# Output projection and gate by result blocks: the last two weight tiles accumulate one 128x512 quarter after the other, and a transpose moves behind the first attention tile

## The chip, the cores and the metric

The kernel runs on one core of a Trainium2 chip. Its time is the device time of one execution in microseconds (us). The engines are TensorE (PE, with its weight loads shown apart as PEld), VectorE (DVE), ScalarE (ACT), GpSimd (POOL) and SyncE (SP), which here only issues DMAs. Each works through its own queue in order and waits on semaphores. PE writes its results to PSUM, which has eight banks of 512 fp32 columns on 128 partitions.

## The reference: what is computed

Two layers on 256 tokens of width 1024. In each layer:

```
h  = rmsnorm(x);  f = h @ w_in + b_in
attn = rmsnorm(sliding_window_attention(f))          # 512 channels
rw   = rwkv7(f): recurrence, group norm, gate        # 512 channels
x  = x + concat[attn, rw] @ w_out                    # output projection
x  = x + peer(rmsnorm(x))                            # 8 heads, top 16 of 128^2 experts
x  = x + (p @ ple_proj) * sigmoid(rmsnorm(x) @ ple_gate)   # gate
```

and a last rmsnorm on the output.

## The kernel before, in words

**Precision and weight tiles.** Every large product is made of three fp32r matmuls, high x high, high x low and low x high, where a weight tile (128x1024) is split into `high` (an ACT cast, L456) and `low` (a DVE or POOL subtraction, L827, L426) and the activations into `hTh` and `hTl`. Weight tiles lie two to a 1 MB slab in a ring of four slabs, which SP fills in order; a slab is loaded when the `low` parts of the slab before it in its place have been made. `high` and `low` have four buffers (`DEEP = 4`), and the tile with number `count` may be cast only when `part_used` says that PE is done with the tile four before it. The tiles in their order within a layer: `in` 0 to 20, `out` 0 to 7, `wq` 0 to 15, 256 expert tiles, `ple` 0 to 9 (two for `p @ ple_proj`, eight for the gate).

**Row projections.** The output projection and the gate both run through `token_rows` (L1315). For each weight tile it waits for the tile's `low` part and issues 12 matmuls of 512 columns (L1327): for both token tiles (128 tokens each) the three products, each into two banks. The result thus lies in four blocks of 128x512, in banks 0 to 3 (n = 0, 1 are token tile 0), and all four are complete only with the last weight tile. `p @ ple_proj` lies in banks 4 to 7.

**Output projection.** Out tiles 0 to 3 multiply the attention's channels, 4 to 7 the recurrence's. PE transposes the recurrence's output for tokens 0 to 127 (`transpose_y(0)`), runs out tiles 0 to 3, transposes tokens 128 to 255 (`transpose_y(1)`, L1549) and releases DVE by `yT_ps`. DVE has the low parts of out tiles 4, 5 and 6 in its queue ahead of its wait for `yT_ps`; then it makes `ytmp` for two channel pairs (L1057 to L1062), ACT casts each (L625), DVE makes each `hTl` (L1066). PE waits for the first `hTl` (`yTr_ready`), runs out tiles 4 and 5, waits for the second and runs 6 and 7. DVE adds the four blocks to `xres` (L1074) after a single wait for the last tile, with the low parts of wq 0 to 2 ahead of that wait.

**Norm.** ACT squares and sums each token tile of `xres` (L465) when `x_ready` has counted its additions, POOL makes the reciprocal root (L395, L396), DVE scales (L832), PE transposes 16 squares of 128x128 (L1292), two to an eviction of ACT (`hTh`, L472) and of DVE (`hTl`, L838). ACT can begin when both token tiles' first channels are transposed. Both engines' `norm` take a function `meanwhile` (tile splits) that they run ahead of their evictions. Behind it PE's `channel_rows` (L1301) runs the `wq` or the next layer's `in` tiles: 24 matmuls of 256 columns (L1311) into one bank.

**Gate.** PE runs `ple` tiles 0 and 1 on `p`, the norm, then tiles 2 to 9. ACT waits once for the last tile and makes four sigmoids (L806), DVE for each block a product (L1271) and an addition to `xres` (L1272). In layer 0 both have the split of the next layer's `in` tile 0 in their queues ahead of that; ACT casts `in` 1 and 2 behind the sigmoids.

The order of every queue is written out by hand. The one wait that the sigmoids have, for example, is

```
act.wait_ge(part_used, projection_tile(L, "ple", KT + 1).count + 1)
```

Of the kernel before, what the change touches and what calls it, by code (L numbers as in the profile page):

```python
# [15 lines left out]
P = 128  # L16
DEPTH, SEQ, D = 2, 256, 1024
TB = SEQ // P
KT = D // P
# [33 lines left out]
DEEP = 4  # L53
# [10 lines left out]
C_GMIX, C_GFFN, C_GPLE, C_BIN, C_MU = 0, 8, 16, 24, 45  # L64
# [70 lines left out]
def hybrid_encoder(nc, x, w_slabs, peer_slabs, vecs, consts, p_t, g_final, out):  # L135
    with ExitStack() as ctx:
        def sem(name):
            return ctx.enter_context(nc.semaphore(name))
# [127 lines left out]
        sumsq, rms, xn_ready, xT_ps, hT_hi, hT_lo = (sem(n) for n in ("sumsq", "rms", "xn_ready", "xT_ps", "hT_hi", "hT_lo"))  # L266
        x_ready = sem("x_ready")

# [174 lines left out]
        def _(act):  # L443
# [7 lines left out]
            def split(tile):  # L451

                if tile.count >= DEEP:
                    act.wait_ge(part_used, tile.count - DEEP + 1)
                act.wait_ge(filled[tile.slab % RING], 16 * fills(tile.layer, tile.slab))
                act.copy(high[:, tile.count % DEEP], raw(tile.slab, tile.half)).then_inc(part_hi, 1)  # L456
# [17 lines left out]
            for L in range(DEPTH):  # L474
                V = vec[:, L]

                def early():
                    if L:
                        split(projection_tile(L, "in", 3))
                    else:  # L480
                        for k in range(2):
                            split(projection_tile(L, "in", k))
                        act.wait_ge(in_v, 16)

                norm(3 * L, V[:, C_GMIX:C_GMIX + KT], early)
                if L == 0:
                    for k in range(2, 4):
                        split(projection_tile(L, "in", k))
                if L == 0:
# [136 lines left out]
                split(projection_tile(L, "out", KT - 1))  # L626
                for k in range(4):
                    split(projection_tile(L, "wq", k))

                norm(3 * L + 1, V[:, C_GFFN:C_GFFN + KT])  # L630

# [170 lines left out]
                if L < DEPTH - 1:  # L802
                    split(projection_tile(L + 1, "in", 0))
                act.wait_ge(part_used, projection_tile(L, "ple", KT + 1).count + 1)
                for n in range(4):
                    act.activation(sgm[:, n // 2, (n % 2) * 512:(n % 2 + 1) * 512], PS[:, n], ACT.Sigmoid).then_inc(sgm_ready, 1)  # L806
                if L < DEPTH - 1:
                    for k in range(1, 3):
                        split(projection_tile(L + 1, "in", k))

# [4 lines left out]
        def _(dve):  # L815
# [28 lines left out]
            for L in range(DEPTH):  # L844
# [223 lines left out]

                for k in range(3):
                    split(projection_tile(L, "wq", k))  # L1070
                dve.wait_ge(part_used, projection_tile(L, "out", KT - 1).count + 1)
                for n in range(4):
                    s = slice((n % 2) * 512, (n % 2 + 1) * 512)
                    ins = dve.tensor_tensor(xres[:, n // 2, s], xres[:, n // 2, s], PS[:, n], ALU.add)  # L1074
                    if n % 2:
                        ins.then_inc(x_ready, 1)
                dve.wait_ge(x_ready, TB * (3 * L + 1))

                norm(3 * L + 1, V[:, C_GFFN:C_GFFN + KT], lambda: split(projection_tile(L, "wq", 3)))

# [184 lines left out]
                if L < DEPTH - 1:  # L1265
                    split(projection_tile(L + 1, "in", 0))
                dve.wait_ge(part_used, projection_tile(L, "ple", KT + 1).count + 1)
                for n in range(4):
# [15 lines left out]
        def _(pe):  # L1284
# [30 lines left out]
            def token_rows(L, stage, k0, hi, lo, ktiles, bank0, norm=None, first=True, last=True):  # L1315

                for k in range(ktiles):
                    tile = projection_tile(L, stage, k0 + k)
                    pe.wait_ge(low_dve, tile.low + 1)
                    if norm is not None:  # L1320

                        pe.wait_ge(hT_lo, KT * (norm + 1))
                    b = tile.count % DEEP
                    for tb in range(TB):
                        for c, (h, w) in enumerate(((hi, high), (hi, low), (lo, high))):
                            for s in range(2):
                                ins = mm(PS[:, bank0 + 2 * tb + s], h[:, k, tb * P:(tb + 1) * P], w[:, b, s * 512:(s + 1) * 512],  # L1327
                                         start=first and k == 0 and c == 0, stop=last and k == ktiles - 1 and c == 2)
                    ins.then_inc(part_used, 1)

            pe.wait_ge(in_c, 16)
            pe.wait_ge(zeros_made, 1)
            for L in range(DEPTH):
# [221 lines left out]

                pe.wait_ge(y_ready, NCHUNK * (L + 1))
                token_rows(L, "out", 0, hTh, hTl, 4, 0, last=False)
                transpose_y(1, yT_ps)
                for n in range(2):
                    pe.wait_ge(yTr_ready, 2 * L + n + 1)  # L1560
                    ks = slice(4 + 2 * n, 6 + 2 * n)
                    token_rows(L, "out", 4 + 2 * n, hTh[:, ks], hTl[:, ks], 2, 0, first=False, last=n == 1)

# [113 lines left out]
                norm(3 * L + 2)  # L1677
                token_rows(L, "ple", 2, hTh, hTl, KT, 0, 3 * L + 2)

# [95 lines left out]
```

## Time and profile before

| | |
|---|---|
| median of 3 runs | 2297.89 us (2294.98 to 2299.03) |
| the profiled execution | 2296.89 us, span of its instructions 2295.1 us |
| busy: PE / DVE / ACT / POOL | 2184.8 / 1604.7 / 1102.1 / 329.4 us |
| chain that ended last, by engine | PE 79%, DVE 7%, POOL 6%, issue 6%, ACT 1% |
| mean granted clock of TensorE | 0.979 |

How to read it: the span goes from the first instruction to the last. The chain is followed back from the last instruction, at each step to what released it. "x48" is a number of instructions; a bracket behind a row of a timeline is the idle time of the engine before it and what ended that.
### The profile page before, as it was taken

To read this page: it belongs to the slowest core of one execution; us is meant where nothing else is said; L and a number is where in the kernel's file an instruction comes from. 1 tells how busy PE (TensorE), PEld (TensorE's weight loads), DVE (VectorE), ACT (ScalarE), POOL (GpSimd) and SP (SyncE) were. 2 spreads that over 40 slices of the span, in tenths; PEclk is the share of its full clock that TensorE was granted. 3 is DMA by queue.
4 is the path that set the end of the run, shared out by engine and by line. 5 is a ranking of instruction groups with operands and counts; after the bars stand their busy time and mean duration, and the time that the engine had idled before them with its cause. 6 is when DMAs were issued, how large, how long until landed. Compare 5 with 4: busy or idle time off the path is not lost.

```text
span 2295.1 us, 55123 instructions
## 1 busy us (share of the span) xinstructions
PE 2184.8 (95%) x21760; PEld 1948.0 (85%) x21760; DVE 1604.7 (70%) x3080; ACT 1102.1 (48%) x1891; POOL 329.4 (14%) x164
## 2 busy tenths in 40 slices
PE   8897999999999999999898889999999999999997
PEld 8786999988888888788696869999888888887885
DVE  6645697786666667975566448978766666679754
ACT  5533455444444444445464334554444444445443
POOL 0020698000000000000000216970000000000000
PEclk9899999999999999999998989999999999999998
DMA  6212345434444444445341123544344444444451
GB/s 250 92 40 75 129 166 184 145 129 164 164 166 167 168 171 157 159 159 190 127 149 73 40 92 129 178 170 147 129 164 164 164 166 166 169 158 154 166 193 63
DMA packets 46617, 335.03 MB, mean 146 GB/s; under 512 B 5168, under 2 KB 5296, under 8 KB 6320
## 3 DMA queue, kind: packets, MB, share of 16 engines
q1 hardware_dynamic: 46512, 333.61, 40.5%
q8 instruction: 68, 1.11, 0.2%
q14 instruction: 37, 0.30, 0.0%
HBM read 332.54 MB, written 1.05 MB: 145 GB/s over the span
## 4 chain that ended last, share of the span: by engine, by line
PE 79%; DVE 7%; POOL 6%; issue 6%; ACT 1%; DMA 0%; POOLq 0%; SPq 0%; DVEq 0%; ACTq 0%
PE PS L1626 31%; PE PS L1603 23%; PE PS L1311 8%; PE PS L1615 6%; POOL low L432 5%; PE PS L1327 4%; PE PS L1518 1%; PE PS L1475 1%; DVE low L1084 1%; PE PS L1509 1%; PE PS L1299 1%; DVE rnorm L943 1%; DVE hot L1154 1%; DVE hot L1150 1%; PE PS L1343 0%
## 5 line engine op out<-in xcount | busy, mean ns | idle before, releaser
L651 ACT CAST high<-ring 128x1024 fp32r<-128x1024 f32 x512 | 535.6, 1048 | 602.7 <-PE PS L1603 444.4
L1603 PE MATMUL PS<-hTh,high 128*128 128x256 f32 x2048 | 594.7, 290 | 12.7 <-ACT GA L655 10.9
L1603 PE MATMUL PS<-hTh,low 128*128 128x256 f32 x2048 | 578.8, 283 | 0.0
L1603 PE MATMUL PS<-hTl,high 128*128 128x256 f32 x2048 | 577.2, 282 | 0.0
L1084 DVE TENSOR_TENSOR low<-ring,high 128x1024 fp32r<-128x1024 f32 x432 | 515.5, 1220 | 0.8 <-ACT high L651 0.6
L1603 PEld LDWEIGHTS PS<-hTh,high 128*128 128x128 f32 x2048 | 387.2, 189 | 17.4 <-ACT GA L655 9.7
L1603 PEld LDWEIGHTS PS<-hTl,high 128*128 128x128 f32 x2048 | 387.5, 189 | 0.0
L1603 PEld LDWEIGHTS PS<-hTh,low 128*128 128x128 f32 x2048 | 387.5, 189 | 0.0
L1626 PE MATMUL PS<-high,WH 128*128 128x512 f32 x1024 | 323.8, 397 | 0.0
L1626 PE MATMUL PS<-low,WH 128*128 128x512 f32 x1024 | 318.0, 392 | 0.0
L1626 PE MATMUL PS<-high,WL 128*128 128x512 f32 x1024 | 316.4, 390 | 0.0
L1147 DVE TENSOR_TENSOR is_i<-iota_half,repeats 128x256 bf16<-128x256 bf16 x256 | 74.3, 290 | 256.4 <-ACT repeats L681 252.3
L395 POOL TENSOR_SCALAR stat<-stat 128x1 f32<-128x1 f32 x14 | 5.0, 356 | 1638.4 <-ACT xn L465 1638.4
L432 POOL TENSOR_TENSOR low<-ring,high 128x1024 fp32r<-128x1024 f32 x80 | 226.4, 2867 | 32.7 <-ACT high L651 32.7
L1626 PEld LDWEIGHTS PS<-high,WL 128*128 128x128 f32 x1024 | 192.2, 188 | 43.0
L1626 PEld LDWEIGHTS PS<-low,WH 128*128 128x128 f32 x1024 | 192.2, 188 | 42.9
L1615 PEld LDWEIGHTS PS<-hot,hot 128*128 128x128 bf16 x6144 | 169.9, 96 | 60.1 <-issue 54.1
L1626 PEld LDWEIGHTS PS<-high,WH 128*128 128x128 f32 x1024 | 179.2, 188 | 26.4
L1615 PE MATMUL PS<-hot,hot 128*128 128x32 bf16 x6144 | 193.9, 177 | 7.6 <-DVE hot L1154 7.6
L672 ACT CAST WH<-GA 128x256 fp32r (+1 forms) x256 | 102.7, 401 | 201.4 <-PE PS L1626 190.9
L1150 DVE TENSOR_TENSOR hot<-iota_half,repeats 128x1024 bf16<-128x1024 bf16 x256 | 175.6, 686 | 0.0
L1311 PE MATMUL PS<-hTh,high 128*128 128x256 f32 x592 | 173.3, 293 | 2.4 <-DVE hTl L838 2.4
(245 smaller groups left out, 3020.5 us busy)
## 6 DMA issues: line engine op xcount, KB each, us to landing
ring<-in_peer_slabs SPq DMA_DIRECT2D x256, 1024.0 KB, 4.8
ring<-in_w_slabs SPq DMA_DIRECT2D x58, 1024.0 KB, 4.8
xres<-in_x SPq DMA_DIRECT2D x2, 512.0 KB, 4.6
out<-obuf SPq DMA_DIRECT2D x2, 512.0 KB, 2.6
cst<-in_consts SPq DMA_DIRECT2D x1, 680.0 KB, 10.5
praw<-in_p_t SPq DMA_DIRECT2D x1, 512.0 KB, 15.1
gfin<-in_g_final SPq DMA_DIRECT2D x1, 512.0 KB, 5.6
vec<-in_vecs SPq DMA_DIRECT2D x1, 356.0 KB, 7.3
```

What stands on the lines that cost most here:

```text
L432: pool.tensor_tensor(low[:, b], ring[:, place, half * D:(half + 1) * D], high[:, b].bitcast(F32), ALU.subtract).then_inc(low_pool, 1)
L651: act.copy(high[:, (c0[L] + j) % DEEP], ring[:, place, half * D:(half + 1) * D]).then_inc(part_hi, 1)
L672: act.copy(WH[:, j % 2:j % 2 + 1], GA[:, bass.ds(place, 1)]).then_inc(w_hi, 1)
L943: dve.reciprocal(rnorm[:], rnorm[:]).then_inc(kk_ready, 1)
L1084: dve.tensor_tensor(low[:, b], ring[:, place, half * D:(half + 1) * D], high[:, b].bitcast(F32), ALU.subtract).then_inc(low_dve, 1)
L1147: dve.tensor_tensor(is_i2[:, b].rearrange("p t (a c) -> p t a c", c=REP), iotas[:, QT // REP * chunk:QT // REP * (chunk + 1)].unsqueeze(1) ...
L1150: dve.tensor_tensor(hot1[:, b].rearrange("p t (a c) -> p t a c", c=REP), iotas.unsqueeze(1).broadcast_to([P, GROUP, NSUB // REP, REP]), re ...
L1311: ins = mm(dst, w[:, b, ks], h[:, k], start=n == 0, stop=n == 3 * KT - 1)
L1327: ins = mm(PS[:, bank0 + 2 * tb + s], h[:, k, tb * P:(tb + 1) * P], w[:, b, s * 512:(s + 1) * 512], start=first and k == 0 and c == 0, sto ...
L1603: ins = mm(PS[:, 6 + j % 2, 0:SEQ], u[:, b, ks], h[:, k], start=n == 0, stop=n == 3 * KT - 1)
L1615: ins = mm(PS[:, 4 + b, t * QT:(t + 1) * QT], hot1[:, b, t], hot2[:, b, part, t], start=part == 0, stop=part == 2)
L1626: ins = mm(PS[:, 2 * tb + s], w[:, j % 2, tb * P:(tb + 1) * P], v[:, b, s * 512:(s + 1) * 512], start=False, stop=False, skip_group_check= ...
```

## The change

1. **Output projection, order on PE.** Out tile 0, then `transpose_y(1)`, then out tiles 1 to 3, where the transposes stood behind tile 3.
2. **Last two tiles by blocks.** A new function `block_after_block` runs the last two weight tiles of the output projection and of the gate. It waits for the later tile's `low` part once and then, for each of the four blocks, issues the six matmuls of both tiles. Each of the first three blocks has a semaphore count (`out_ps`, `gate_ps`); with the last block both tiles count as used (`part_used`). The number of matmuls and of weight loads is as before. For the output projection both halves of `hTl` are now awaited ahead of the first block; each of tiles 4 and 5 still waits for the first half alone.
3. **DVE and ACT, block by block.** DVE waits for each block ahead of its addition, ACT for each block ahead of its sigmoid.
4. **Splits moved.** `wq` 2 and 3 can be cast only when the blocks are done: ACT casts them in the norm, between the squares and the evictions; DVE makes the low part of `wq` 2 there and that of `wq` 3 behind its evictions. In the gate of layer 0, ACT casts `in` 1 and 2 of the next layer between the next norm's squares and evictions, and `in` 3 behind the evictions; DVE's order there is unchanged.

```diff
--- before.py
+++ after.py
@@ -264,7 +264,7 @@
         zeros_made = sem("zeros_made")
 
         sumsq, rms, xn_ready, xT_ps, hT_hi, hT_lo = (sem(n) for n in ("sumsq", "rms", "xn_ready", "xT_ps", "hT_hi", "hT_lo"))
-        x_ready = sem("x_ready")
+        x_ready, out_ps, gate_ps = (sem(n) for n in ("x_ready", "out_ps", "gate_ps"))
 
         bq_ready, in_evac, mixed = (sem(n) for n in ("bq_ready", "in_evac", "mixed"))
         vtA_ps, vtA_ready, sc_ps, lg_made, nm_ready, p_ready = (sem(n) for n in ("vtA_ps", "vtA_ready", "sc_ps", "lg_made", "nm_ready", "p_ready"))
@@ -476,16 +476,16 @@
 
                 def early():
                     if L:
-                        split(projection_tile(L, "in", 3))
+                        for k in range(1, 3):
+                            split(projection_tile(L, "in", k))
                     else:
                         for k in range(2):
                             split(projection_tile(L, "in", k))
                         act.wait_ge(in_v, 16)
 
                 norm(3 * L, V[:, C_GMIX:C_GMIX + KT], early)
-                if L == 0:
-                    for k in range(2, 4):
-                        split(projection_tile(L, "in", k))
+                for k in range(3 if L else 2, 4):
+                    split(projection_tile(L, "in", k))
                 if L == 0:
                     act.wait_ge(in_p, 16)
                     act.copy(pTh[:], praw[:]).then_inc(p_hi, 1)
@@ -624,10 +624,14 @@
                     act.wait_ge(yg_ready, 2 * L + n + 1)
                     act.copy(hTh[:, 4 + 2 * n:6 + 2 * n], ytmp[:, 2 * n:2 * n + 2]).then_inc(yTr_hi, 1)
                 split(projection_tile(L, "out", KT - 1))
-                for k in range(4):
+                for k in range(2):
                     split(projection_tile(L, "wq", k))
 
-                norm(3 * L + 1, V[:, C_GFFN:C_GFFN + KT])
+                def rest():
+                    for k in range(2, 4):
+                        split(projection_tile(L, "wq", k))
+
+                norm(3 * L + 1, V[:, C_GFFN:C_GFFN + KT], rest)
 
                 def scores_out(m):
                     act.wait_ge(psc_ps, HC * L + m + 1)
@@ -801,12 +805,12 @@
                 act.activation(ahead, minus_half, ACT.Sigmoid)
                 if L < DEPTH - 1:
                     split(projection_tile(L + 1, "in", 0))
-                act.wait_ge(part_used, projection_tile(L, "ple", KT + 1).count + 1)
                 for n in range(4):
+                    if n < 3:
+                        act.wait_ge(gate_ps, 3 * L + n + 1)
+                    else:
+                        act.wait_ge(part_used, projection_tile(L, "ple", KT + 1).count + 1)
                     act.activation(sgm[:, n // 2, (n % 2) * 512:(n % 2 + 1) * 512], PS[:, n], ACT.Sigmoid).then_inc(sgm_ready, 1)
-                if L < DEPTH - 1:
-                    for k in range(1, 3):
-                        split(projection_tile(L + 1, "in", k))
 
             norm(3 * DEPTH, None)
 
@@ -1066,17 +1070,21 @@
                     dve.tensor_tensor(hTl[:, ks], ytmp[:, 2 * n:2 * n + 2], hTh[:, ks].bitcast(F32), ALU.subtract).then_inc(yTr_ready, 1)
                 split(projection_tile(L, "out", KT - 1))
 
-                for k in range(3):
+                for k in range(2):
                     split(projection_tile(L, "wq", k))
-                dve.wait_ge(part_used, projection_tile(L, "out", KT - 1).count + 1)
                 for n in range(4):
                     s = slice((n % 2) * 512, (n % 2 + 1) * 512)
+                    if n < 3:
+                        dve.wait_ge(out_ps, 3 * L + n + 1)
+                    else:
+                        dve.wait_ge(part_used, projection_tile(L, "out", KT - 1).count + 1)
                     ins = dve.tensor_tensor(xres[:, n // 2, s], xres[:, n // 2, s], PS[:, n], ALU.add)
                     if n % 2:
                         ins.then_inc(x_ready, 1)
                 dve.wait_ge(x_ready, TB * (3 * L + 1))
 
-                norm(3 * L + 1, V[:, C_GFFN:C_GFFN + KT], lambda: split(projection_tile(L, "wq", 3)))
+                norm(3 * L + 1, V[:, C_GFFN:C_GFFN + KT], lambda: split(projection_tile(L, "wq", 2)))
+                split(projection_tile(L, "wq", 3))
 
                 def split_tile(count, j, place, half):
                     dve.wait_ge(part_hi, c0[L] + 1 + count)
@@ -1264,7 +1272,6 @@
                     split(projection_tile(L, "ple", k))
                 if L < DEPTH - 1:
                     split(projection_tile(L + 1, "in", 0))
-                dve.wait_ge(part_used, projection_tile(L, "ple", KT + 1).count + 1)
                 for n in range(4):
                     s = slice((n % 2) * 512, (n % 2 + 1) * 512)
                     dve.wait_ge(sgm_ready, 4 * L + n + 1)
@@ -1327,6 +1334,22 @@
                                 ins = mm(PS[:, bank0 + 2 * tb + s], h[:, k, tb * P:(tb + 1) * P], w[:, b, s * 512:(s + 1) * 512],
                                          start=first and k == 0 and c == 0, stop=last and k == ktiles - 1 and c == 2)
                     ins.then_inc(part_used, 1)
+
+            def block_after_block(L, stage, k0, hi, lo, done):
+
+                tiles = [projection_tile(L, stage, k0 + k) for k in range(2)]
+                pe.wait_ge(low_dve, tiles[1].low + 1)
+                for n in range(4):
+                    rows, cols = slice(n // 2 * P, (n // 2 + 1) * P), slice(n % 2 * 512, (n % 2 + 1) * 512)
+                    for k, tile in enumerate(tiles):
+                        b = tile.count % DEEP
+                        mm(PS[:, n], hi[:, k, rows], high[:, b, cols], start=False, stop=False)
+                        mm(PS[:, n], hi[:, k, rows], low[:, b, cols], start=False, stop=False)
+                        ins = mm(PS[:, n], lo[:, k, rows], high[:, b, cols], start=False, stop=k == 1)
+                        if n == 3:
+                            ins.then_inc(part_used, 1)
+                    if n < 3:
+                        ins.then_inc(done, 1)
 
             pe.wait_ge(in_c, 16)
             pe.wait_ge(zeros_made, 1)
@@ -1554,12 +1577,13 @@
 
 
                 pe.wait_ge(y_ready, NCHUNK * (L + 1))
-                token_rows(L, "out", 0, hTh, hTl, 4, 0, last=False)
+                token_rows(L, "out", 0, hTh, hTl, 1, 0, last=False)
                 transpose_y(1, yT_ps)
-                for n in range(2):
-                    pe.wait_ge(yTr_ready, 2 * L + n + 1)
-                    ks = slice(4 + 2 * n, 6 + 2 * n)
-                    token_rows(L, "out", 4 + 2 * n, hTh[:, ks], hTl[:, ks], 2, 0, first=False, last=n == 1)
+                token_rows(L, "out", 1, hTh[:, 1:4], hTl[:, 1:4], 3, 0, first=False, last=False)
+                pe.wait_ge(yTr_ready, 2 * L + 1)
+                token_rows(L, "out", 4, hTh[:, 4:6], hTl[:, 4:6], 2, 0, first=False, last=False)
+                pe.wait_ge(yTr_ready, 2 * (L + 1))
+                block_after_block(L, "out", 6, hTh[:, 6:8], hTl[:, 6:8], out_ps)
 
                 norm(3 * L + 1)
 
@@ -1675,7 +1699,8 @@
                     pe.wait_ge(p_lo, 1)
                 token_rows(L, "ple", 0, pTh[:, L], pTl[:, L], 2, 4)
                 norm(3 * L + 2)
-                token_rows(L, "ple", 2, hTh, hTl, KT, 0, 3 * L + 2)
+                token_rows(L, "ple", 2, hTh, hTl, KT - 2, 0, 3 * L + 2, last=False)
+                block_after_block(L, "ple", KT, hTh[:, KT - 2:KT], hTl[:, KT - 2:KT], gate_ps)
 
 
 def shape_constants():
```

## Rows read from the trace of the kernel before

**Rows 1.** The chain that ended last, share of the span by line (page).

```profile
PE PS L1626 31%; PE PS L1603 23%; PE PS L1311 8%; PE PS L1615 6%; POOL low L432 5%; PE PS L1327 4%; PE PS L1518 1%; PE PS L1475 1%; DVE low L1084 1%; PE PS L1509 1%; PE PS L1299 1%; DVE rnorm L943 1%; DVE hot L1154 1%; DVE hot L1150 1%; PE PS L1343 0%
```

**Rows 2.** Waits, whole span: waiter, releaser: total us, times, longest.

```profile
...
PE PS L1292 <- DVE xn L832: 24.3, 6, 8.0
...
PE PS L1327 <- DVE hTl L1066: 11.1, 2, 5.5
```

**Rows 3.** Chain, layer 0, output projection and norm: start us, us, what.

```profile
...
182.59 11.35 PE PS L1327 x48
193.94 0.96 PE PS L1549 x30
...
200.39 13.29 PE PS L1327 x48
...
218.04 2.36 PE PS L1292 x10
...
221.93 6.12 PE PS L1311 x48
```

**Rows 4.** Timeline, DVE, same stretch: start, us, operation, idle before.

```profile
...
184.15 0.43 DVE L1017 TENSOR_TENSOR yc<-yc,stat 128x256 f32<-128x256 f32 x1
...
192.27 1.23 DVE L827 TENSOR_TENSOR low<-ring,high 128x1024 fp32r<-128x1024 f32 x1 [1.56 <-ACT high L456]
194.93 0.99 DVE L1057 TENSOR_SCALAR ytmp<-PS,vec 128x256 f32<-128x256 f32 x2 [1.43 <-PE PS L1549]
...
209.21 1.23 DVE L827 TENSOR_TENSOR low<-ring,high 128x1024 fp32r<-128x1024 f32 x1 [1.56 <-ACT high L456]
...
213.70 2.48 DVE L1074 TENSOR_TENSOR xres<-xres,PS 128x512 f32<-128x512 f32 x4 [0.48 <-PE PS L1327]
```

**Rows 5.** Timeline, ACT, the same stretch.

```profile
...
213.70 1.04 ACT L456 CAST high<-ring 128x1024 fp32r<-128x1024 f32 x1 [1.74 <-PE PS L1327]
...
216.22 1.06 ACT L465 ACTIVATE xn<-xres 128x1024 f32<-128x1024 f32 x1
...
220.42 3.03 ACT L472 ACTIVATE hTh<-PS,vec 128x256 fp32r<-128x256 f32 x8 [3.06 <-PE PS L1292]
```

**Rows 6.** Timeline, DVE, layer 0's gate and the norm behind it.

```profile
...
1136.77 1.23 DVE L827 TENSOR_TENSOR low<-ring,high 128x1024 fp32r<-128x1024 f32 x1 [6.09 <-ACT high L456]
1140.28 0.69 DVE L1271 TENSOR_TENSOR ptmp<-sgm,PS 128x512 f32<-128x512 f32 x1 [2.29 <-ACT sgm L806]
...
1144.97 0.71 DVE L1272 TENSOR_TENSOR xres<-xres,ptmp 128x512 f32<-128x512 f32 x1
...
1147.86 0.75 DVE L832 TENSOR_SCALAR xn<-xres,stat 128x1024 f32<-128x1024 f32 x1 [1.39 <-POOL stat L396]
```

**Rows 7.** Chain, layer 1, output projection and norm.

```profile
...
1338.88 14.02 PE PS L1327 x48
...
1358.77 0.70 PE PS L1292 x2
...
1361.01 7.72 PE PS L1311 x48
```

**Rows 8.** DMA issues (page): KB each, us to landing.

```profile
...
ring<-in_w_slabs SPq DMA_DIRECT2D x58, 1024.0 KB, 4.8
```

**Rows 9.** Timeline, ACT, layer 0's gate.

```profile
...
1139.58 2.06 ACT L806 ACTIVATE sgm<-PS 128x512 f32<-128x512 f32 x4 [2.84 <-PE PS L1327]
```

**Rows 10.** Chain, layer 1's gate.

```profile
...
2257.53 24.93 PE PS L1327 x96
...
2287.88 0.70 DVE xres L1272
```

**Rows 11.** Windows: length; busy (instructions) by engine; granted clock; DMA share; GB/s.

```profile
...
218.00:222.00 4.00, 3.70 (x17) 3.33 (x17) 2.59 (x4) 1.58 (x5) 0.63 (x2) 0.57 0.13 16
222.00:258.00 36.00, 36.00 (x305) 36.00 (x305) 17.31 (x105) 17.30 (x34) 23.58 (x10) 1.00 0.39 145
```

**Rows 12.** Instructions of L1327: duration ns min/median/max, first and last start, forms.

```profile
...
L1327 PE MATMUL PS<-high,hTh x128: 390/395/796, 182.5 to 2281.1; 128*128 128x512 f32 x128
```

## The prediction

> **What bounds the kernel.** I read the chain of waits first. TensorE (PE) holds 79% of it, most in the expert stage (L1626, L1603) and the column projections (L1311), which the edit leaves alone [rows 1]. The table of waits then shows PE idle mainly in the norms, until VectorE (DVE) has scaled a token tile (24.3 us in six waits), and 11.1 us, in two, ahead of the last output-projection tiles [rows 2]. Nothing else covers such a pause, so what shortens one moves all that follows. I read the four places touched (output projection and gate of both layers) engine by engine. Below, E is the end of a projection's last matmul, E' its end after the change; "block" is one 128x512 quarter of the result.
>
> **Early transposes (twice).** In layer 0 PE takes 48 matmuls for four weight tiles in 11.35 us (0.2365 each, 2.84 a tile), transposes for 0.96, then waits until 200.39 [rows 3]. After the change the transposes stand behind tile 0, at 182.59 + 2.84 = 185.4. Their input is complete at 184.15 + 0.43 = 184.6, so they don't stall [rows 4]. The work is only moved. But DVE, first to read the transposes, has the low parts of out tiles 4 to 6 ahead of that in its queue. The last of these starts at 192.27 and takes 1.23; it follows ScalarE's (ACT) cast of that tile, which waits for PE to finish tile 2, and tile 2 now ends 0.96 later. So DVE is free at 192.27 + 1.23 + 0.96 = 194.46, where it now starts at 194.93 [rows 4]. Of the 5.5 us pause only 0.47 goes; the late thing next is DVE itself, whose seven steps up to the first hTl are unchanged. Nearest bounds: 0, and 1.43 if DVE's whole wait there went [rows 4]. I take 0.47, twice, 0.94 in all. The second wait, now ahead of the blocks, is long over: both hTl end at 201.1, two tiles before the blocks begin.
>
> **Output projection by blocks, with norm.** E is 200.39 + 13.29 = 213.68 in layer 0 [rows 3]. Blocks end at E' minus 4.26, 2.84, 1.42 and 0 (six matmuls of 0.2365). DVE's queue has the low part of wq tile 1 ahead of the additions: 209.21 + 1.23 - 0.47 = 209.97, which is E' - 3.24. Additions run at 0.62 (2.48 for four) [rows 4]: two end by E' - 1.9, the third by E' - 0.7, and only the fourth (0.68 to its end) stands behind E'. Now four stand there, with the two squares of ACT in a row behind the first pair: the second square starts at 216.22, E + 2.54 [rows 5]. After the change it starts at E' + 0.7.
>
> From the last update of xres to DVE's second scaling is 2.18 us, read where the first square is long done, as it will be here: 1144.97 + 0.71 to 1147.86 [rows 6]. So that scaling starts at E' + 2.88 and ends at E' + 3.63. Two transposes until ACT may read follow (0.70 in layer 1 [rows 7], which I take; ten in a row took 2.36 in layer 0 [rows 3], so 0.47 is the lower end). ACT starts at about E' + 4.39, and from there to PE's first wq matmul it was 221.93 - 220.42 = 1.51 [rows 3, 5]. That gives E' + 5.90, against 221.93 - 213.68 = 8.25 in layer 0 and 1361.01 - 1352.90 = 8.11 in layer 1 [rows 3, 7]. The eight transposes of the first token tile are ready from E' + 1.5 and done by E' + 3.4 at the 0.236 of layer 0's ten: covered. Saved: 2.35 and 2.21, sum 4.56.
>
> What is moved: tiles 6 and 7 now free their buffers together, at E', so ACT's casts of wq 2 and 3 (1.04 each [rows 5]) go behind the second square: E' + 1.9 to E' + 4.0, still ahead of its eviction at 4.39. DVE's low part of wq 2 (1.23) goes from E' + 3.6 to 4.8, ahead of hTl, which waits for ACT's second eviction at about E' + 5.3: hidden by 0.5; without that cover it costs up to 0.7. wq 3 goes behind the eight hTl, done at about E' + 10, while PE needs it three tiles after 5.9, at about E' + 15. SyncE's queue has one load waiting on that low part (wq 10 and 11), and all later ones behind it. It would start about 2.4 us later than now and land 4.8 later [rows 8], near E' + 15; PE comes to that tile after ten tiles of about 3.3, near E' + 39. POOL's queue has only its two norm steps earlier. No cost.
>
> **Gate of layer 0.** E is 1139.56, just ahead of the first sigmoid at 1139.58 [rows 9]; the first block would be ready at 1135.3. But ACT casts next-layer tile 0 ahead of the sigmoids and DVE makes its low part from 1136.77 to 1138.00 [rows 6]; neither moves, since both wait for a weight load and not for PE. So DVE's gate chain starts at 1138.02, where it now starts at 1140.28 behind that sigmoid [rows 6, 9]. Its four steps take 1.35 each (1140.28 to 1145.68), the last block's sigmoid is there at 1140.2 and the chain reaches it only at 1142.1. It ends 2.26 us earlier, and the norm behind it follows unchanged. Tiles 1 and 2 of the next layer are cast between the second square (until 1144.6) and the first eviction (1147.1): 2.1 us into a hole of 2.5. Cover gone, 0.4. Tile 3 is behind the evictions and needed 9 us later. I take 2.26. Its bounds are 0, if the chain should start no earlier, and the 4.0 of the next paragraph, where no such low part is in the way.
>
> **Gate of layer 1.** Nothing is cast ahead. E is 2257.53 + 24.93 = 2282.46 and the last update ends at 2288.58, E + 6.12 [rows 10]. After: block n is ready at E - 4.2, -2.8, -1.4, 0, a sigmoid adds 0.7, a DVE step takes 1.35. These keep pace with PE, and the last ends at E + 0.7 + 1.39 = E + 2.09. ACT in order: last sigmoid until E + 0.6, first square until 1.9, second square at 2.1. The first output multiplication, a DVE pass over 128x1024 like a low part's 1.23, goes from about E + 2.9 and is over before the second can start at E + 4.27. Saved: 4.03.
>
> **Sum.** 0.94 + 4.56 + 2.26 + 4.03 = 11.8 us. The profiled execution took 2296.89 (span 2295.1, 1.8 around it), so 2285.1; against the median of the runs shown, which is 1.0 above it, 2286.1. That is the forecast.
>
> **Same-bank rule.** In a block six matmuls of 512 columns run into one PSUM bank, where they now change banks each time. The nearest row is the wq stage: 24 of 256 columns in one bank, at 305 in 36 us, 0.118 each [rows 11], half of 0.2365 for half the columns. I take no cost. "TensorE: Matmul & The Clock Gate", section "Step-by-step: what each phase is for", in the Trainium skill, says that the drain of one matmul overlaps the filling of the next, so the distance is the number of columns; by this too nothing is added, and the rival below would be void. No row has 512 columns in one bank.
>
> **Rivals.** (a) *Clock falls more often.* After a pause the granted clock is 0.57, near the lower level (1.2 GHz), from 218 to 222, then 1.00 [rows 11]. Behind such pauses 48 matmuls took 13.29 and 14.02 instead of 11.35, and the first 48 of wq 6.12 or 7.72 [rows 3, 7]. My pauses are shorter (PE restarts 1.5 us after E' rather than 4.4) but in more pieces, and the first tiles after them come sooner, so they may fall inside the slow stretch. If layer 0's wq becomes like layer 1's (+1.6), next-layer tile 0 likewise (+1.6) and one output projection (+0.7), it is 3.9 worse: 2290.0. The same page of the Trainium skill, section "A second HAM failure mode: psum-queue depth-cycling", has this as a rule: small idles between groups make the clock swing and the re-warming eats the throughput.
> (b) *Clock stays up* through the shorter norms: layer 1's first 48 of wq fall to layer 0's 6.12, a further 1.6: 2284.5. For it: less idle. Against: every pause over 4 us here was followed by a slow stretch.
> (c) *Slower: same-bank matmuls can't overlap.* If each took the 0.395 us of its own record [rows 12] instead of 0.2365, 96 of them add 15.2: 2301.3. It decides from 11.8 / 96 = 0.123 a matmul. Against: the one-bank rate of [rows 11].
> (d) *Not passed on.* The three inner gains end in a stage paced by something that does not move with PE, and only the tail's 4.0 is kept: 2293.9. Against: every load of the ring waits for a low part, which waits for PE.
>
> **How the numbers follow.** Forecast 0.74, (a) 0.10, (b) 0.07, (c) 0.04, (d) 0.05. The range goes from 2283, below (b), to 2291, above (a), which leaves out (c), (d) and a little of the rest. A measurement of this kernel tells some 0.2% (4.6 us, so 2293.3) from no change. Faster: 0.91; same, which is (d): 0.05; slower, (c): 0.04.
>
> **What would show it.** PE's pause ahead of out tile 4 about 5.0 us and not 5.5, with the transposes at 185.4; first wq matmul 5.9 us behind the last block; one addition behind each; the gate chain of layer 0 starting right behind the low part of next-layer tile 0; the last update of layer 1 at E + 2.1. Block matmuls 0.2365 apart refute (c). Wrong if the pause ahead of tile 4 shrinks by over 1 us, if PE stalls at the moved transposes, or if the first 48 wq matmuls of layer 0 take over 7 us.

## The result and the profile after

The changed kernel took 2284.64 us in the median of four runs against 2298.46 for the kernel before, ratio 0.9939 (95% interval 0.9922 to 0.9957). Two further comparisons of five runs each gave 0.9955 (0.9941 to 0.9969) and 0.9952 (0.9939 to 0.9965). So it is faster by 0.45 to 0.6%, 10 to 14 us. The two profiled executions took 2296.89 and 2285.02 us, spans 2295.1 and 2283.2. What follows explains those 11.9 us.

Lines have moved: matmuls of the row projections L1327 to L1334 (blocks: L1346 to L1348), transposes of the recurrence's output L1549 to L1572, of the norm L1292 to L1299, column projections L1311 to L1318.

The chain through layer 0's output projection and norm, after (start us, us, what), beside [rows 3]:

```profile
182.37 2.98 PE PS L1334 x12
185.35 0.91 PE PS L1572 x30
186.25 5.79 PE PS L1334 x24
192.06 1.06 ACT high L456
...
194.28 1.00 DVE ytmp L1061 x2
...
199.74 7.31 PE PS L1334 x24
...
212.39 0.24 PE PS L1348
...
216.32 0.47 PE PS L1299 x2
...
218.32 6.70 PE PS L1318 x48
```

The transposes sit at 185.35 and don't stall. The chain leaves PE at 192.06: it goes over ACT's cast and VectorE's low part of out tile 6 to `ytmp` at 194.28 (the cast waits for PE to finish tile 2, whose buffer it takes). What is late is now VectorE's queue, not the transposes. From PE's first out tile to its first wq tile it was 221.93 - 182.59 = 39.34 and is 218.32 - 182.37 = 35.95.

VectorE's timeline of the same stretch (operation, idle before it and its releaser), beside [rows 4]:

```profile
208.17 1.23 DVE L831 TENSOR_TENSOR low<-ring,high 128x1024 fp32r<-128x1024 f32 x1 [1.57 <-ACT high L456]
209.31 1.28 DVE L1081 TENSOR_TENSOR xres<-xres,PS 128x512 f32<-128x512 f32 x2
211.27 0.69 DVE L1081 TENSOR_TENSOR xres<-xres,PS 128x512 f32<-128x512 f32 x1 [0.69 <-PE PS L1348]
212.65 0.69 DVE L1081 TENSOR_TENSOR xres<-xres,PS 128x512 f32<-128x512 f32 x1 [0.69 <-PE PS L1348]
...
215.51 0.75 DVE L836 TENSOR_SCALAR xn<-xres,stat 128x1024 f32<-128x1024 f32 x1 [1.39 <-POOL stat L396]
216.18 1.22 DVE L831 TENSOR_TENSOR low<-ring,high 128x1024 fp32r<-128x1024 f32 x1
```

One addition stands behind PE's last block, the second scaling starts 2.9 us behind it and the low part of wq 2 fits ahead of the evictions, as in the prediction.

The chain in layer 1, beside [rows 7]:

```profile
1334.44 8.18 PE PS L1334 x24
...
1347.97 0.25 PE PS L1348
...
1351.91 0.45 PE PS L1299 x2
...
1353.89 6.12 PE PS L1318 x48
```

Layer 0's gate on VectorE, beside [rows 6]:

```profile
1134.85 1.23 DVE L831 TENSOR_TENSOR low<-ring,high 128x1024 fp32r<-128x1024 f32 x1 [5.94 <-ACT high L456]
1135.99 0.68 DVE L1278 TENSOR_TENSOR ptmp<-sgm,PS 128x512 f32<-128x512 f32 x1
...
1140.68 0.69 DVE L1279 TENSOR_TENSOR xres<-xres,ptmp 128x512 f32<-128x512 f32 x1
```

The products start right behind the low part of the next layer's tile 0. At the very end of the kernel, beside [rows 10] (VectorE):

```profile
2275.33 0.69 DVE L1279 TENSOR_TENSOR xres<-xres,ptmp 128x512 f32<-128x512 f32 x1
2276.89 1.28 DVE L1287 SCALAR_TENSOR_TENSOR obuf<-xres,stat,gfin 128x1024 f32<-128x1024 f32 x1 [0.86 <-POOL stat L396]
```

and POOL there:

```profile
2277.29 0.96 POOL L395 TENSOR_SCALAR stat<-stat 128x1 f32<-128x1 f32 x1 [0.54 <-ACT xn L465]
```

All 11.9 us by stage, each within its own profile. Stretches go from start to start; "last update" is the end of the last addition to `xres`:

| stretch | before | after | difference |
|---|---|---|---|
| layer 0, first out tile to first wq tile | 39.34 | 35.95 | -3.39 |
| layer 0, first 48 wq matmuls | 6.12 | 6.70 | +0.58 |
| layer 0, gate: expert result added, to first tile of layer 1 | 46.90 | 45.01 | -1.89 |
| layer 1, first out tile to first wq tile | 39.93 | 36.82 | -3.11 |
| layer 1, first 48 wq matmuls | 7.72 | 6.12 | -1.60 |
| layer 1, gate: expert result added, to last update of xres | 42.41 | 38.46 | -3.95 |
| last update to the end | 6.52 | 7.17 | +0.65 |
| everything else (some 1950 us) | | | +0.8 |

Of the last row 0.65 lies in one place, the first 192 matmuls of layer 1's `in` tiles, right behind the gate's norm (before, then after):

```profile
1150.90 23.21 PE PS L1311 x192
1146.59 23.86 PE PS L1318 x192
```

### The profile page after: what moved, and what is told of

Its sections match the earlier page's. It is cut to its first block, busy times and chain, and to the rows that moved or that the text cites. A ratio compares the mean times of both kernels' runs of the same rounds, so it can differ in the third digit from the quotient of the medians.

```text
span 2283.2 us, 55117 instructions
## 1 busy us (share of the span) xinstructions
PE 2185.3 (96%) x21760; PEld 1946.3 (85%) x21760; DVE 1604.7 (70%) x3080; ACT 1102.3 (48%) x1891; POOL 329.4 (14%) x164
## 4 chain that ended last, share of the span: by engine, by line
PE 78%; DVE 7%; issue 6%; POOL 6%; ACT 2%; DMA 1%; SPq 0%; POOLq 0%; ACTq 0%; DVEq 0%
PE PS L1650 31%; PE PS L1627 23%; PE PS L1318 8%; PE PS L1639 6%; POOL low L432 5%; PE PS L1334 3%; PE PS L1541 1%; PE PS L1498 1%; DVE low L1092 1%; PE PS L1532 1%; DMA praw<-in_p_t 1%; PE PS L1306 1%; ACT high L456 1%; DVE rnorm L947 1%; DVE hot L1162 1%
## 5 line engine op out<-in xcount | busy, mean ns | idle before, releaser
L1318 PE MATMUL PS<-hTh,high 128*128 128x256 f32 x592 | 172.3, 291 | 3.8 <-DVE hTl L842 2.9
## 6 DMA issues: line engine op xcount, KB each, us to landing
cst<-in_consts SPq DMA_DIRECT2D x1, 680.0 KB, 10.3
```

What stands on the lines that cost most here:

```text
L1318: ins = mm(dst, w[:, b, ks], h[:, k], start=n == 0, stop=n == 3 * KT - 1)
```

## Experiments

Ratios are to the kernel before on the same chip, with 95% intervals.

**The whole again, and its three parts.** Each part undoes the others' edits.

```diff
# a_after: the changed kernel
# b_transposes_only: before, with
-                token_rows(L, "out", 0, hTh, hTl, 4, 0, last=False)
+                token_rows(L, "out", 0, hTh, hTl, 1, 0, last=False)
                 transpose_y(1, yT_ps)
+                token_rows(L, "out", 1, hTh[:, 1:4], hTl[:, 1:4], 3, 0, first=False, last=False)
# c_out_blocks_only: after, less b and less the gate's blocks, waits and in splits
# d_gate_blocks_only: after, less b and less the output projection's blocks, waits and wq splits
```

> The changed kernel beside the three parts of it. Theory 1 (only the pieces that stand behind a projection's last matmul got shorter, and they add up): 11.8 us faster than before, the sum of the three parts. Theory 2 (part of the gain is TensorE's clock, which in the profile after stayed at 1.00 through layer 1's norm and the first 48 wq matmuls, 6.12 us instead of 7.72): 12 to 14 us faster, more than the durations alone give, and with it a sum of the parts that differs from the whole by a microsecond or two, since each part leaves other pauses.

> Only the transposes move behind out tile 0; all else as before. Theory 1: the pause ahead of out tile 4 goes from 5.5 to 5.0 us in both layers, since VectorE still has the low parts of tiles 4 to 6 in its queue: 0.9 us faster in all. Rival: VectorE's whole 1.43 us wait for the transposes goes, and the clock comes back sooner: 2.9 us faster or more.

> Only the output projection's last two tiles by blocks, with the additions and the wq splits that go with them; transposes and gate as before. Theory 1: PE's first wq matmul comes 5.7 to 5.9 us behind the last block instead of 8.1 to 8.25, 4.6 to 5.0 us faster. Theory 2: 1.6 us more in the layer whose first 48 wq matmuls run at the full clock, 6.2 to 6.6.

> Only the gate's last two tiles by blocks, with the sigmoids and the in splits that go with them; output projection as before. Theory 1: layer 0 2.3 us, bounded by the low part of the next layer's tile 0, and layer 1 4.0 us: 6.3 faster. If the 0.7 us that the profile after shows more behind the last update (POOL's first step 0.96 us instead of 0.22) belongs to this part: 5.6 faster.

| | median | ratio |
|---|---|---|
| before | 2294.76 | |
| whole (a) | 2285.18 | 0.9955 (0.9941 to 0.9969) |
| transposes (b) | 2293.22 | 0.9996 (0.9987 to 1.0005) |
| out blocks (c) | 2289.47 | 0.9979 (0.9970 to 0.9988) |
| gate blocks (d) | 2288.21 | 0.9973 (0.9962 to 0.9983) |

The ratios give -0.9, -4.8 and -6.2 us, together -11.9, and -10.3 for the whole, whose interval (-13.5 to -7.1) holds the sum. The differences of the medians are -1.5, -5.3 and -6.6, together -13.4, and -9.6 for the whole. So the parts add up as far as the intervals can tell. The transposes by themselves can't be told from no change in time; their pause can be read in the chain of b, layer 0:

```profile
186.40 5.80 PE PS L1327 x24
...
199.90 12.89 PE PS L1327 x48
```

PE restarts 17.40 us after its first out tile (182.50), where it was 200.39 - 182.59 = 17.80. That is the 0.4 to 0.5 of theory 1, and not 1.4. In c the first 48 wq matmuls took 6.12 and 6.11 in the two layers. But the slow 7.72 of before is gone as well in layer 1 of b (6.27) and of d (6.12), which run the last two out tiles and the additions as before. So that the blocks removed it, as theory 2 has it, is not shown, and c's ratio, at the 4.8 of theory 1, can't separate the two. In d POOL's first step for the second token tile at the end took 0.96 us, as in every profile of the whole change; in b and c it took 0.22, as before. The loss at the end belongs to the gate's blocks, though d's interval holds both the 6.3 and the 5.6 of its expectation.

What the clock leaves open can be read from the profiles of this comparison, of a2 (the change again) and of the result. Each number is the time of the same matmuls in one execution:

| profile | first 48 of wq, layers 0 and 1 | gate's 96, layer 0 | first 192 of layer 1's `in` |
|---|---|---|---|
| before | 6.12, 7.72 | 24.20 | 23.21 |
| b | 6.12, 6.27 | 25.03 | 23.43 |
| c | 6.12, 6.11 | 25.12 | 23.21 |
| d | 6.21, 6.12 | 24.84 | 23.93 |
| the change | 6.70, 6.12 | 24.82 | 23.86 |
| a | 6.16, 6.16 | 24.94 | 23.87 |
| a2 | 6.12, 6.13 | 25.00 | 23.97 |

Only the last column follows the kernel: 23.2 to 23.4 without the gate's blocks, 23.9 to 24.0 with them. In the first two the one profile of before stands alone with 7.72 and 24.20, and the 6.70 of the change is 6.16 and 6.12 in a and a2.

**VectorE's order.** If its queue holds PE, turning it round must pay, and only with the early transposes.

```diff
# e_values_first: the change, and on VectorE
-                split(projection_tile(L, "out", 4))
-                for k in range(5, KT - 1):
-                    split(projection_tile(L, "out", k))
                 dve.wait_ge(yT_ps, 2 * (L + 1))
...              (ytmp and both hTl, unchanged)
-                split(projection_tile(L, "out", KT - 1))
+                for k in range(4, KT):
+                    split(projection_tile(L, "out", k))
# on ScalarE
-                split(projection_tile(L, "out", 4))
-                for k in range(5, KT - 1):
-                    split(projection_tile(L, "out", k))
                 for n in range(2):
+                    split(projection_tile(L, "out", 4 + n))
                     act.wait_ge(yg_ready, 2 * L + n + 1)
                     act.copy(hTh[:, 4 + 2 * n:6 + 2 * n], ...)
-                split(projection_tile(L, "out", KT - 1))
+                for k in range(6, KT):
+                    split(projection_tile(L, "out", k))
# f_values_first_late_transposes: e, with transpose_y(1) behind out tile 3 again
```

> The changed kernel, with VectorE's queue turned round: it makes ytmp and both hTl as soon as the transposes behind out tile 0 are there, and the low parts of out tiles 4 to 6 after that; ScalarE casts tile 4, the first half of hTh, tile 5, the second half, then tiles 6 and 7. Theory 1 (VectorE's order, not the transposes, holds PE for 4.9 us ahead of out tile 4): the seven steps run under out tiles 1 to 3, the pause goes in both layers (9.8 us), and with it the slow stretch behind it (48 matmuls 12.9 and 13.8 us in the profile after, 11.2 at the full rate, 4.3 together): 14 us faster than the change, about 2271. Rival: the low parts of tiles 4 and 5 come too late instead, and the pause only moves: within 2 us of the change.

> VectorE's queue turned round as in the kernel that took 2271.25, but with the transposes behind out tile 3, as before the change. If the moved transposes bring something only together with VectorE's order, the order alone loses: ytmp can't start before 195.2, and the low part of tile 4, now behind both hTl, is ready 7.4 us after PE's transposes and not 4.9: about 5 us slower than the change, 2290. Rival (the order alone makes the gain): 2271 again.

e took 2271.25 us (before: 2295.35), ratio 0.9899 (0.9886 to 0.9913), 12 to 14 us faster than the change. The change itself was timed in other comparisons; g below, which is the change with one operation moved, took 2284.05 beside e. f took 2289.7, 0.9974 (0.9964 to 0.9984): 5.4 slower than the change beside it (2284.27). Both came as expected. The chain of e, layer 0:

```profile
183.10 3.00 PE PS L1331 x12
186.09 0.91 PE PS L1569 x30
187.00 14.15 PE PS L1331 x60
```

60 matmuls without a pause, at 0.236 each: out tiles 1 to 5. VectorE in the same run starts on `ytmp` 0.1 us behind the transposes, and makes the low parts of the next tiles only after that, still in time (the second row is a merged one: both hTl end at 193.27, then the low parts of tiles 4 to 7 follow):

```profile
187.07 0.99 DVE L1057 TENSOR_SCALAR ytmp<-PS,vec 128x256 f32<-128x256 f32 x2 [2.00 <-PE PS L1569]
...
193.18 4.73 DVE L830 TENSOR_TENSOR low<-ring,high 128x1024 fp32r<-128x1024 f32 x4
```

In f the low parts of tiles 4 and 5 start at 201.79, and PE, done with its transposes at 195.66, waits for the first until 203.16:

```profile
194.71 0.95 PE PS L1569 x30
...
203.16 8.23 PE PS L1331 x24
```

**TensorE's clock.** The pause stays, but PE is kept busy in it.

```diff
                 token_rows(L, "out", 1, hTh[:, 1:4], hTl[:, 1:4], 3, 0, first=False, last=False)
+                keep_warm(6, 10)      # i_warm; i2_warm_five: keep_warm(6, 5)
```

> The changed kernel with ten matmuls on zeros, 0.43 us each, in PE's pause ahead of out tile 4 (nothing reads them). The pause stays, only PE is busy in it. Clock theory: the next 48 matmuls take 11.2 instead of 12.9 and 13.8 us, 3 to 4 us faster than the change. Rival (the slow stretch has another cause, or the extra matmuls push the real ones back): no gain.

> The changed kernel with five matmuls on zeros in PE's pause ahead of out tile 4 in place of ten: the run with ten showed that each takes 0.86 us and not 0.43, so that they outlasted the pause of 4.9 us by 3.7 in both layers. Five take 4.3 and fit. Clock theory: the pause as in the change, the 48 matmuls behind it 11.2 us (as with ten) instead of 12.9 and 13.8: 3 to 4 us faster than the change. Rival: no gain.

Ten took 8.58 us and not 4.3, so i_warm was slower than the change: 2290.1, 0.9977 (0.9968 to 0.9986). Its expectation missed by the size of a matmul on fp32 zeros (0.86). Five fit (from the first out tile to tile 4 it is 17.40, and 17.37 in the change), and i2_warm_five took 2285.27, 0.9955 (0.9942 to 0.9968): no gain over 2284.27, where 3 to 4 us were expected. Its chain, layer 0 and layer 1:

```profile
200.33 5.86 PE PS L1334 x24
...
217.48 7.49 PE PS L1318 x48
...
1336.06 5.84 PE PS L1334 x24
...
1353.43 7.84 PE PS L1318 x48
```

The out tiles behind the pause ran close to the full rate (5.86 and 5.84 for 24, where the change had 7.31 and 8.18 and 24 times 0.2365 is 5.68). The pause is as long as in the change and only PE's activity in it differs, so it is the slow clock that had stretched them. But in this execution the first 48 wq matmuls took 7.49 and 7.84 instead of 6.70 and 6.12: of 3.8 us, 2.5 were given back. The 1.3 that are left are less than the two intervals (3 us each way) can show. The granted clock of that run (windows: length, busy by engine, clock, DMA share, GB/s):

```profile
196.00:200.00 4.00, 3.68 (x9) 1.33 (x7) 3.90 (x7) 0.91 (x2) 0.00 (x0) 1.00 0.07 29
200.00:204.00 4.00, 3.67 (x16) 3.00 (x17) 2.19 (x3) 1.85 (x3) 0.00 (x0) 1.00 0.16 18
218.00:222.00 4.00, 4.00 (x24) 4.00 (x23) 3.21 (x7) 1.00 (x3) 0.00 (x0) 0.62 0.02 4
```

And of the change, for layer 0 and layer 1, beside [rows 11]:

```profile
200.00:204.00 4.00, 4.00 (x12) 3.15 (x13) 1.69 (x2) 0.68 (x1) 0.00 (x0) 0.63 0.18 57
218.00:222.00 4.00, 3.74 (x25) 3.71 (x25) 4.00 (x9) 1.85 (x6) 0.00 (x0) 0.75 0.00 0
1354.00:1360.00 6.00, 6.00 (x50) 6.00 (x51) 3.62 (x8) 2.74 (x6) 1.41 (x1) 1.00 0.20 57
```

That the fillers moved the slow stretch to the next pause is not shown. With ten of them, in i_warm, the out tiles ran at the full rate and so did the wq tiles behind the norm, in both layers:

```profile
203.22 5.57 PE PS L1334 x24
...
220.06 6.12 PE PS L1318 x48
...
1340.62 5.58 PE PS L1334 x24
...
1357.45 6.12 PE PS L1318 x48
```

And e and j_all (below), which have neither the pause nor fillers, took 6.12 and 6.12, and 6.12 and 7.83. What decides whether the clock falls in the norm stays open.

**What bounds layer 0's gate, and POOL at the end.**

```diff
# g_next_tile_late: the change; on VectorE split(in 0 of the next layer) moves
# from ahead of the gate chain to between the norm's two scalings
# h_output_in_quarters: the change, and
+                for h in range(1 if tb else 4):
+                    s = slice(0, D) if tb else slice(h * 256, (h + 1) * 256)
+                    ins = dve.scalar_tensor_tensor(obuf[:, tb, s], xres[:, tb, s], rstd[:, tb:tb + 1], gfin[:, s], ALU.mult, ALU.mult)
+                ins.then_inc(out_ready, 1)
# j_all: e and h; ScalarE casts in 0 behind the first two sigmoids,
# VectorE makes its low part in the next norm, ahead of in 1's
```

> The changed kernel, with the low part of next-layer tile 0 taken out of VectorE's queue ahead of layer 0's gate chain and put between the two scalings of the norm. If that low part (and the weight load before it) is what bounds layer 0's gate, as the prediction has it, the chain starts behind the first sigmoid and keeps pace with PE: 1.5 to 2 us faster than the change. The sigmoids still wait for ScalarE's cast of that tile. Rival: the first sigmoid or PE bounds the chain anyway: no change.

> The changed kernel, with the first output multiplication at the very end in four pieces of 256 columns. In the profile after, POOL's first step for the second token tile took 0.96 us instead of 0.22 and ended when VectorE's 1.28 us multiplication did. If POOL's small step can't run while such a VectorE instruction does, it ends here with a piece, and takes 0.6 us or less. Rival (chance, or the pace of POOL itself): 0.9 to 1.0 again.

> The kernel that took 2271.25, with the output multiplication in quarters and, in layer 0's gate, ScalarE's cast of the next layer's tile 0 behind the first two sigmoids and its low part on VectorE in the next norm, next to that of tile 1. With the low part alone moved the chain started 0.5 us sooner and nothing was gained: the first sigmoid still waited for a cast that waited for a weight load. Now the chain keeps pace with PE's blocks and its last update is 2.1 us behind the last of them instead of 3.6; two low parts in a hole of 1.7 us cost 0.7 of that. Expected: 1 to 1.5 us faster than 2271.25, of which 0.4 from the quarters.

g took 2284.05, 0.9953 (0.9940 to 0.9965): no gain, where 1.5 to 2 was expected. Its chain:

```profile
1128.96 4.86 DMA ring<-in_w_slabs
...
1133.90 1.05 ACT high L456
1134.94 0.51 ACT sgm L813
...
1142.13 0.74 POOL stat L395
```

The sigmoids still waited for the cast and that for the weight load, so the products started 0.5 us sooner and not 2. The 0.5 went into POOL's first step, 0.74 us instead of the 0.22 it had in the change, while VectorE made the moved low part beside it (1141.56 to 1142.78).

h was executed only once (2282.08), so its time tells nothing. POOL's first step there, beside the 0.96 above:

```profile
2274.77 0.22 POOL L395 TENSOR_SCALAR stat<-stat 128x1 f32<-128x1 f32 x1 [0.54 <-ACT xn L465]
```

With VectorE's operation in pieces POOL's step takes 0.22 us. So it was held by the long VectorE operation, and is not slow by itself. The pieces have a price, 1.67 us for four where one operation took 1.28, so the time behind the last update goes from 7.17 to 6.8 and not back to 6.52.

j_all, the best kernel, took 2270.0 us (before: 2295.13), 0.9886 (0.9872 to 0.9900), that is 14 to 15 us faster than the change beside it (2284.27). In its layer 0 PE's last block ends 0.02 ahead of the last sigmoid at 1133.17, and the last update is 2.06 behind it, where it was 1141.38 - 1137.77 = 3.6 in the change:

```profile
1134.52 0.69 DVE L1275 TENSOR_TENSOR xres<-xres,ptmp 128x512 f32<-128x512 f32 x1
```

e and j were not timed in one comparison and their intervals overlap, so that j's further edits gain the expected 1 to 1.5 us is not shown by time. In the profiles, layer 0's gate from its last block to layer 1's first tile is 1.0 shorter than in e, and the end 0.5, as expected. Yet the profiled execution of j took 1.0 us longer than that of e (2271.1 against 2270.06): its first 48 wq matmuls in layer 1 took 7.83 us where e's took 6.12.

## Why the prediction was right, point by point

**Forecast: 11.8 us less, 2286.1.** Measured 2284.64, and -11.9 between the profiled executions. The mechanism was right. That the sum came out to 0.1 us is luck. The four terms gave 0.86, 4.99, 1.89 and 3.95, together 11.7, because two misses of 0.4 cancelled. Outside the sum -1.60 and -0.65 (layer 1's wq, the out tiles behind the pauses) met +0.58, +0.65 and +0.8 (layer 0's wq, the end, all else), and the -1.60 belongs to one slow stretch in the one profile of before.

**Early transposes, 0.94.** The pauses shrank by 0.43 in each layer. That VectorE's queue bounds here was the main point of this step; b, e and f show it from three sides.

**Behind the output projection, 4.56.** Measured 8.25 to 5.70 and 8.11 to 5.67: 4.99. Each is 0.2 more than forecast because the first two transposes took 0.47 and 0.45, the lower end of the bound, where I had taken 0.70.

**Gate of layer 0, 2.26.** Measured 1.89. One clause failed, on the cast and the low part of next-layer tile 0: "neither moves, since both wait for a weight load and not for PE". The load waits for the low part of the last gate tile, and this for PE to free a buffer. The gate's 96 matmuls took 24.82 instead of 24.20, and the whole chain of load, cast and low part came 0.5 later (the low part 21.90 behind the first gate matmul, where it was 21.42). This is not the change: in b and c, whose gate is as before, the 96 took 25.03 and 25.12. The bound itself was right, but incomplete: g showed that ScalarE's cast holds it as well, and only j, which moves both, reached E + 2.06.

**Gate of layer 1, 4.03.** Measured 3.95. E to the last update was forecast 2.09 and was 2.07.

**Not in the sum: the end.** 0.65 was lost behind the last update. I had fitted the first output multiplication into a hole of VectorE, but not looked at POOL, whose step runs in that same hole and was held until the multiplication was over (2276.89 + 1.28 = 2278.17, POOL's step ended at 2278.25). The row for this was in the trace of before, as 0.61 instead of 0.22 us for the same step next to a scaling, and I had not used it (VectorE, then POOL):

```profile
217.23 0.75 DVE L832 TENSOR_SCALAR xn<-xres,stat 128x1024 f32<-128x1024 f32 x1 [1.05 <-POOL stat L396]
217.45 0.61 POOL L395 TENSOR_SCALAR stat<-stat 128x1 f32<-128x1 f32 x1 [0.33 <-ACT xn L465]
```

**Rivals.** (a) came true in part, and small: the first 192 matmuls of layer 1's `in` tiles are 0.4 to 0.8 slower in all three profiles of the change than in before, b and c. Layer 0's first wq tiles were 0.58 slower in the first profile of the change, nearly so in g and h, which are the change in that place (6.51 and 6.74), but not in a and a2 (6.16 and 6.12). (b) can't be told from chance. Layer 1's first 48 did take 6.12 and not 7.72, but so they did in d, whose output projection is as before. The 0.65 by which the out tiles behind the pauses shrank (13.29 and 14.02 to 12.88 and 13.78) is no more than the spread among the profiles that run the last two out tiles as before (b: 12.89 and 14.22, d: 14.15 and 13.47). (c) is refuted by the chain: every block matmul into the same bank is 0.23 apart, as with alternating banks. (d) is refuted by the table, where all else changed by +0.8 us, and by c, where the output projection's blocks alone gave 4.8 (2.8 to 6.9).

## What to carry to other kernels

When an earlier result hardly shortens a pause, look at what stands in the queue of the engine that reads it: here the moved transposes shortened the pauses by 0.9 us by themselves, and the kernel by some 13 us more once VectorE (and ScalarE with it) took them ahead of work that had time, while that order without the moved transposes lost 5 us. Where a result is finished block by block, count what is still behind the last block, and look at the small step of a third engine too. A slow stretch of the clock that one profile shows and another doesn't must not be booked as a gain or a loss of a change: profile the same kernel more than once.

## What the runs showed of the hardware

- A POOL operation on one column (0.22 us) took 0.96, 0.74 and 0.61 us when a VectorE operation over 1024 columns had started just before it, ended with it each time, and took 0.22 when that operation came in pieces of 256 columns. The Trainium skill, page "SBUF — State Buffer", section "SBUF: two separate sides", has such a rule: VectorE and GpSimd share a pair of SBUF ports, and whichever instruction starts first holds it to its end, if VectorE's has two inputs in SBUF or runs in a mode that uses both ports. The trace agrees: the three POOL steps ended 0.08 us behind the VectorE operation (2278.17, 1142.78, 217.98 against 2278.25, 1142.87, 218.06). The first two VectorE operations have two wide inputs in SBUF; the third has one, and no row names its mode. Beside a product that reads PSUM the step was not held (the change, layer 0's gate, VectorE and POOL):

```profile
1139.96 0.68 DVE L1278 TENSOR_TENSOR ptmp<-sgm,PS 128x512 f32<-128x512 f32 x1
1139.99 0.22 POOL L395 TENSOR_SCALAR stat<-stat 128x1 f32<-128x1 f32 x1 [33.38 <-ACT xn L465]
```

- With PE kept busy through a pause the granted clock was 1.00 behind it (200 to 204 in i2, where the change had 0.63), and 24 matmuls took 5.86 us instead of 7.31. Behind the next pause it was 0.62 in i2 (218 to 222) and 0.75 in the change, while in i_warm it stayed 1.00 (218 to 222) and the 48 wq matmuls took 6.12 us. The same kernel differs there from one execution to the next (6.70, 6.16 and 6.12 in three profiles of the change).
- A matmul of 512 columns on fp32 operands shows as two records and took 0.86 us, against 0.23 for one in fp32r (i_warm, ten in 8.58).
